# Two float32 transformer blocks on one core: the second mixer's heads, turns and diff chain placed at other chunks and banks

## The chip, the cores and the metric

One NeuronCore of one Trainium2 chip runs the whole program in one launch. The metric is the device time of one execution in microseconds (us). The times shown are those of three executions.

## What is computed

The input is 256 tokens by 2048 columns in float32. A first block (attention and retention, gated and merged, then a gated FFN) is followed by a second one. Cut to what the change touches, the second is:

```python
h = rmsnorm(x, attn_pre_norm)
gq, gk, gv, gg, ga, dq, dk, dv = split(h @ w_in)
o_a = rmsnorm(gla_chunked(gq, gk, gv, log_a), gla_norm) * silu(gg)  # 4 gated heads, 128 by 256
o_b = rmsnorm(diff_attention(dq, dk, dv, lam), diff_norm) * (1 - lambda_init)  # 4 diff heads
x = x + rmsnorm(concat(o_a, o_b) @ w_o, attn_post_norm)
h = rmsnorm(x, ffn_pre_norm)
a, b = split(h @ w_ffn_in)
x = x + rmsnorm((gelu(conv3(a)) * b) @ w_ffn_out, ffn_post_norm)

# diff_attention, each head: (softmax(q1 k1) - lam * softmax(q2 k2)) @ v, causal
```

## The kernel before

The weights are streamed: each block of 512 output columns is eight **chunks** of 512 KB, which SP's queue loads into four slots of `raw`. ACT rounds a chunk to `whi` (L887), DVE subtracts to get the rest `wlo` (L1377), and TensorE multiplies both with the turned activations `hT`, which are held as a high and a low part too (`cols_block`, L377 and L378, or `rows_block` and `tall_block`, L388 to L390, twelve matmuls a chunk in the latter). A slot is free for the next load when DVE has read it, and `whi` is free when TensorE has used the chunk. So ACT and DVE split chunk c+4 right after TensorE has finished chunk c.

All other work is hung into this stream by hand. Every engine has its own program, in which a function `side(c)` or `side(k)` is called after chunk c (or after the split that belongs to it), and `linear_attention(c, h)`, `head_norms(pos)` or `diff_attention(pos)` say by their `if` what happens after which chunk. Nothing is reordered by a scheduler; engines meet at semaphores alone, and an engine that waits in a side holds back the splits or the matmuls that stand behind it.

PSUM has eight banks `ps[:, 0..7]`. The running block owns two or four of them, and side work has the rest. A **turn** (`turn_group`, L455 on TensorE, L931 or L934 on ACT, L1422 or L1426 on DVE) transposes 256 columns of rows into `hT`; TensorE's turn of a group waits by `evicted` until DVE is through with the bank. The eight groups of the second mixer's output (`turn_group(5, ...)`) are four from the gated heads, done in bank 2 (the fourth in bank 0), and one from each diff head, in bank 3.

- A gated head (`linear_attention`) has two halves, t = 0 and 1: decay sums on TensorE (L750), `Exp` on ACT, products on DVE (L1820), scores on TensorE (L757), masked and summed by DVE (L1829 to L1833, the copy L1837 last). Heads 0 to 2 lie beside the blocks `gg0`, `gv1`, `gg1`, head 3 beside the first `dv` block, one chunk later. `linear_out` (L772) multiplies with the values, `norm_gla` and `head_out` scale the head's rows.
- A diff head (`diff_attention`), pos counting chunks from the second `dv` block on: scores (L813) at pos 2+4h, top on DVE, `Exp` on ACT (L1268) at 3+4h, probabilities on DVE (L1901 to L1910) at 4+4h, their turn (L803) at 6+4h, output (L826) at 7+4h, its norm on ACT and DVE (L1879) at 8+4h and 9+4h, its turn at 10+4h. From pos 8 on this lies beside the output projection `o2`.
- Rows are scaled late: `late_scale` on DVE makes a diagonal of token scales (L1448) at k = 3, and TensorE spreads it with one product (L492 in the first block, L468 elsewhere) after chunk 5. It needs a `Sqrt` on ACT (`root`, L966), for which ACT first loads a table.
- The attention heads' norms (`head_norms`, L523, ACT L1003, DVE L1520 to L1528) stand after chunks 1, 5, 9 and 13 of the two `va` blocks.
- At the entry of the last FFN DVE adds the normed mixer rows to `resid` (L1994, in four pieces) before each pair of turns, with `m_gain` (L1930) ahead of pieces 2 and 3.

## Time and profile before

| | |
|---|---|
| median of three runs | 2634.39 us (2633.48 to 2635.44) |
| the profiled execution | 2634.3 us, span 2632.5 us |
| busy share of the span | PE 99%, PEld (weight loads) 87%, DVE 60%, ACT 50%, POOL 2% |
| granted TensorE clock, mean | 0.997 of full |
| chain that ended last | PE 95%, DVE 2%, ACT 2% |
| DMA | 192 GB/s read over the span, 62.8% of the 16 engines' span in the main queue |

"Busy" is the time in which at least one instruction of the engine was under way. Matmuls overlap, since each one's record reaches over the start of the next. The chain of waits is followed back from the last instruction to whatever released each step.

### The profile page before, as it was taken

The numbers are of one execution on the slowest core, as the hardware profiler recorded it, in microseconds if no ns is written. First come the engines' busy times: TensorE is split into PE (matmuls) and PEld (weight loads), VectorE is DVE, ScalarE is ACT, GpSimd is POOL, SyncE is SP. The second block draws the span as 40 slices with busy tenths as digits, with TensorE's granted clock in tenths as the row PEclk, the third lists the DMA queues.
The fourth block names the chain that finished last, engine by engine and source line by source line (L and its number), as shares of the span: only waits on it lengthen the run. The fifth ranks groups of instructions, "written<-read, shape, count | busy, mean of one in ns | idle before, by whom it ended". The sixth has DMA issues, their size and how long they took to land.

```text
span 2632.5 us, 37229 instructions
## 1 busy us (share of the span) xinstructions
PE 2593.8 (99%) x13324; PEld 2291.8 (87%) x13324; DVE 1582.7 (60%) x1682; ACT 1310.1 (50%) x1543; POOL 50.8 (2%) x45
## 2 busy tenths in 40 slices
PE   8999999999999999999999999998999999999998
PEld 7988888888888888888888888897889999998887
DVE  5558655556655544545455557666677777766555
ACT  5445655554445444444444455545554444444444
POOL 0000000000000000000000000000000000000000
PEclk9999999999999999999999999999999999999999
DMA  7665665677666666666666655564556666666664
GB/s 237 199 200 174 184 185 173 188 211 226 196 197 191 198 200 195 199 198 199 198 202 202 207 161 165 170 192 128 187 174 203 200 196 199 201 205 202 204 200 159
DMA packets 233270, 507.28 MB, mean 193 GB/s; under 512 B 15829, under 2 KB 18229, under 8 KB 232548
## 3 DMA queue, kind: packets, MB, share of 16 engines
q1 hardware_dynamic: 231712, 499.31, 62.8%
q0 software_dynamic: 1344, 6.81, 0.8%
q8 instruction: 54, 0.88, 0.1%
q14 instruction: 28, 0.23, 0.0%
q10 hardware_dynamic: 132, 0.03, 0.0%
HBM read 504.00 MB, written 2.10 MB: 192 GB/s over the span
## 4 chain that ended last, share of the span: by engine, by line
PE 95%; DVE 2%; ACT 2%; issue 0%; DVEq 0%; ACTq 0%
PE ps L388 21%; PE ps L390 21%; PE ps L389 21%; PE ps L377 19%; PE ps L378 9%; DVE wlo L1377 1%; PE ps L455 1%; ACT whi L887 1%; PE ps L757 0%; PE ps L691 0%; ACT hT L934 0%; PE ps L523 0%; ACT big L959 0%; DVE hT L1426 0%; PE ps L750 0%
## 5 line engine op out<-in xcount | busy, mean ns | idle before, releaser
L1377 DVE TENSOR_TENSOR wlo<-raw,whi 128x1024 fp32r<-128x1024 f32 x944 | 1170.9, 1244 | 984.0 <-ACT whi L887 976.7
L887 ACT ACTIVATE whi<-raw 128x1024 fp32r<-128x1024 f32 x944 | 998.6, 1059 | 1253.3 <-PE ps L390 872.5
L377 PE MATMUL ps<-hT,whi 128*128 128x512 f32 x2304 | 758.0, 383 | 8.1 <-DVE wlo L1377 4.2
L388 PE MATMUL ps<-whi,hT 128*128 128x512 f32 x1792 | 692.8, 387 | 2.7 <-ACT big L992 1.5
L389 PE MATMUL ps<-wlo,hT 128*128 128x512 f32 x1792 | 680.1, 380 | 0.0
L390 PE MATMUL ps<-whi,hT 128*128 128x512 f32 x1792 | 679.9, 379 | 0.0
L378 PE MATMUL ps<-hT,wlo 128*128 128x256 f32 x2304 | 628.0, 273 | 0.0
L377 PEld LDWEIGHTS ps<-hT,whi 128*128 128x128 f32 x2304 | 435.4, 189 | 70.7 <-issue 6.9
L378 PEld LDWEIGHTS ps<-hT,wlo 128*128 128x128 f32 x2304 | 442.3, 192 | 0.1
L388 PEld LDWEIGHTS ps<-whi,hT 128*128 128x128 f32 x1792 | 339.4, 189 | 53.3 <-issue 3.4
L389 PEld LDWEIGHTS ps<-wlo,hT 128*128 128x128 f32 x1792 | 339.5, 189 | 48.8 <-issue 2.6
L390 PEld LDWEIGHTS ps<-whi,hT 128*128 128x128 f32 x1792 | 339.3, 189 | 48.3
L388 PE MATMUL ps<-whi,split_e 128*128 128x512 f32 x832 | 316.4, 380 | 0.2 <-DVE area_d L1713 0.2
L389 PE MATMUL ps<-wlo,split_e 128*128 128x512 f32 x832 | 315.3, 379 | 0.0
L390 PE MATMUL ps<-whi,split_e 128*128 128x512 f32 x832 | 315.3, 379 | 0.0
L388 PEld LDWEIGHTS ps<-whi,split_e 128*128 128x128 f32 x832 | 157.3, 189 | 22.6 <-DVE area_d L1713 0.6
L390 PEld LDWEIGHTS ps<-whi,split_e 128*128 128x128 f32 x832 | 157.2, 189 | 22.3
L389 PEld LDWEIGHTS ps<-wlo,split_e 128*128 128x128 f32 x832 | 157.3, 189 | 22.0
L2104 POOL TENSOR_TENSOR big<-area_d 128x1024 f32 x11 | 34.2, 3111 | 426.8 <-DVE area_d L1457 426.8
L1426 DVE SCALAR_TENSOR_TENSOR hT<-ps,gains,hT 128x256 fp32r<-128x256 f32 x64 | 27.5, 478 | 16.5 <-ACT hT L934 16.5
L934 ACT ACTIVATE hT<-ps,gains 128x256 fp32r<-128x256 f32 x64 | 26.2, 472 | 22.0 <-PE ps L455 21.8
L2015 DVE SCALAR_TENSOR_TENSOR area_d<-temp,conv,area_d 128x256 f32<-128x256 f32 x88 | 36.7, 480 | 0.0
(248 smaller groups left out, 1009.2 us busy)
## 6 DMA issues: line engine op xcount, KB each, us to landing
raw<-w_ffn_in SPq DMA_DIRECT2D x352, 512.0 KB, 3.7
raw<-w_in SPq DMA_DIRECT2D x304, 512.0 KB, 4.3
raw<-w_ffn_out SPq DMA_DIRECT2D x176, 512.0 KB, 4.5
raw<-w_o_ret SPq DMA_DIRECT2D x32, 512.0 KB, 4.5
raw<-w_out SPq DMA_DIRECT2D x32, 512.0 KB, 4.6
raw<-w_o SPq DMA_DIRECT2D x32, 512.0 KB, 3.7
raw<-w_o_attn SPq DMA_DIRECT2D x16, 512.0 KB, 4.5
resid<-x SPq DMA_DIRECT2D x8, 256.0 KB, 5.9
```

The source lines that it names most:

```text
L377: pe.matmul(acc, whi[:, c % SLOTS, f], in_turn(hT[:, kt, :, :]), start=(kt == 0), stop=False)
L378: mm = pe.matmul(acc[:, 0:SEQ], wlo[:, c % SLOTS, f], in_turn(hT[:, kt, 0, :]), start=False, stop=(kt == KT - 1))
L388: pe.matmul(acc, hi, w_hi, start=start, stop=False)
L389: pe.matmul(acc, hi, w_lo, start=False, stop=False)
L390: return pe.matmul(acc, lo, w_hi, start=False, stop=stop)
L455: mm = pe.transpose(ps[:, bank, k2 * SEQ + t * P:k2 * SEQ + t * P + P], src[:, t, (2 * j + k2) * P:(2 * j + k2 + 1) * P], ident)
L887: act.activation(whi[:, c % SLOTS, :], raw[:, c % SLOTS, :], ACT.Copy).then_inc(hi_ready, 1)
L934: ins = act.activation(dst[:, 2 * j + k2, 0, :], src[:, k2, :], ACT.Copy, scale=gains[:, col0 + 2 * j + k2:col0 + 2 * j + k2 + 1])
L1377: dve.tensor_tensor(wlo[:, c % SLOTS, :], raw[:, c % SLOTS, :], whi[:, c % SLOTS, :].bitcast(F32), ALU.subtract).then_inc(lo_ready, 1)
L1426: ins = dve.scalar_tensor_tensor(dst[:, kt, 1, :], src[:, k2, :], gains[:, col0 + kt:col0 + kt + 1], dst[:, kt, 0, :].bitcast(F32), ALU.mu ...
L2015: ins = dve.scalar_tensor_tensor(dst, src, w, dst, ALU.mult, ALU.add)
L2104: pool.tensor_tensor(hidden[:, bass.ds(4 * i, 4), :], up4, prod, ALU.mult).then_inc(S(f"hidden{u}"), 1)
```

## The change

The arithmetic is the same, and so is the work of each engine, except that ACT loads 38 tables where it loaded 41 in the program's text. What moves:

1. **Root tables ahead.** `root_ready()` is a `Sqrt` of one element, put where ACT loads the table before it is wanted: ahead of the first turn, after the `oa` blocks, and ahead of the last but one `fo` block.
2. **Token scales a chunk later.** TensorE's L492 and L468 come after chunk 6 instead of chunk 5.
3. **`head_norms` a chunk later**, on all three engines (DVE's first `head_squares(0)` stays).
4. **First entry of the second mixer.** ACT and DVE turn groups 0 to 3 in one go, and ACT's squares of pieces 0 and 1 come after them.
5. **Gated heads 2 and 3** do their second half one chunk earlier (`gla_again` is 3 instead of 4), and the last head's `linear_out` comes one chunk earlier, `norm_gla` on ACT two and `head_out` on DVE one.
6. **Diff chain.** Turns of the gated rows at pos 1 to 4 in banks 4 and 5 alternately; scores at 3+4h, turn of probabilities at 7+4h, output at 8+4h, turn of the output at 12+4h in bank 2; the other steps one chunk later too.
7. **Entry of the last FFN.** DVE adds piece 1 to `resid` ahead of two splits, computes the `m_gain` of pieces 2 and 3 after the turn before, and turns group 4 ahead of adding piece 3.

```diff
             return 4 if h < 3 else 0
+
+        def gla_again(h):
+
+            return 4 if h < 2 else 3
         def out_bank(h):
...
                             turn_group(u, src, j, 4 + j % 4, j // 2 + (2 if u == 6 and j else 1), max(0, j - 3))
-                    if u in TURNED_SCALE and c == CPB - 3:
+                    if u in TURNED_SCALE and c == CPB - 2:
                         pe.wait_ge(S("diag"), TURNED_SCALE.index(u) + 1)
                         pe.matmul(ps[:, 4, 0:SEQ], ones, scale_diag, start=True, stop=True).then_inc(S("scale"), 1)
...
+                if c == CPB - 2:
                     pe.wait_ge(S("ones_in"), 16)
                     pe.wait_ge(S("diag"), 1)
                     pe.matmul(ps[:, 4, 0:SEQ], ones, scale_diag, start=True, stop=True).then_inc(S("scale"), 1)
-                if c == CPB - 2:
                     pe.wait_ge(S("gains_in"), 16 * 5)
                     pe.wait_ge(S("lambdas_in"), 16 * 4)
                     turn_gains(16, GAIN_ROWS, 5)
...
             def head_norms(pos):
-                if pos == 1:
+                if pos == 2:
                     pe.wait_ge(acc_freed, base["va"] + 1)
-                if pos % 4 == 1:
+                if pos % 4 == 2:
                     head_sum(pos // 4, 4)
-                if pos == 1:
+                if pos == 2:
...
             def linear_attention(c, h):
-                bank = gla_bank(h)
-                if c in (0, 4):
-                    t = c // 4
+                bank, again = gla_bank(h), gla_again(h)
...
             def diff_attention(pos):
+                if pos == 0:
+                    linear_out(G_HEADS - 1)
                 if pos == 1:
-                    linear_out(G_HEADS - 1)
-                for h in at(pos, 6):
+                    pe.wait_ge(acc_freed, base["dv"] + 2)
+                if 1 <= pos <= 4:
+                    turn_group(5, rows_d, pos - 1, 4 + (pos - 1) % 2, pos, evicted=max(0, pos - 2))
+                for h in at(pos, 7):
                     pe.wait_ge(S("d_p"), h + 1)
-                    pe.wait_ge(S("turned5"), 3)
+                    if h > 1:
+                        pe.wait_ge(S("turned5"), 3 + h)
                     for kt, t in ((0, 0), (0, 1), (1, 1)):
                         mm = pe.transpose(ps[:, 2, kt * SEQ + t * P:kt * SEQ + t * P + P],
                                           diff[:, (t + kt) * P:(t + kt + 1) * P], ident)
                     mm.then_inc(S("d_turn"), 1)
-                for h in at(pos, 2):
-                    if h:
-                        pe.wait_ge(S("turned5"), 4)
-                    else:
-                        pe.wait_ge(acc_freed, base["dv"] + 1)
+                for h in at(pos, 3):
                     for c in range(2):
                         for t in range(NT):
                             mm = pe.matmul(ps[:, c, t * P:t * P + (t + 1) * P], tiles_a[:, 2 * h + c, t * P:t * P + P],
                                            tiles_a[:, 8 + 2 * h + c, 0:(t + 1) * P], start=True, stop=True)
                     mm.then_inc(S("d_score"), 1)
-                if pos in (2, 3, 4):
-                    turn_group(5, rows_d, pos - 2, 2, pos - 1, evicted=pos - 2)
-                if pos == 5:
-                    pe.wait_ge(S("d_top"), 1)
-                    turn_group(5, rows_d, 3, 0, 4)
-                for h in at(pos, 7):
+                for h in at(pos, 8):
                     pe.wait_ge(S("d_pT"), h + 1)
-                    pe.wait_ge(S("turned5"), 4 + h)
                     pe.wait_ge(S("rows5"), 4 + h)
                     v = [dv[:, kt, h * SEQ:(h + 1) * SEQ] for kt in range(NT)]
                     pe.matmul(ps[:, 3, 0:SEQ], dT[:, 0:P], v[0], start=True, stop=True)
                     pe.matmul(ps[:, 3, SEQ:], dT[:, P:SEQ], v[0], start=True, stop=False)
                     pe.matmul(ps[:, 3, SEQ:], dT[:, SEQ + P:], v[1], start=False, stop=True).then_inc(S("d_o"), 1)
-                for h in at(pos, 10):
-                    turn_group(5, rows_d, 4 + h, 3, 5 + h)
+                for h in at(pos, 12):
+                    pe.wait_ge(S("d_pT"), min(h + 2, D_HEADS))
+                    turn_group(5, rows_d, 4 + h, 2, 5 + h)
             def last_gla(c):
                 if c == 1:
...
                     if n == 0:
+                        pe.wait_ge(S("turned5"), 4)
                         acc_free(base["o2"], hc == 1)
                         return
                     for kept in ("m_kept0", "m_kept1"):
...
+            def root_ready():
+
+                act.activation(warm, eps["one"], ACT.Sqrt)
+
             def resid_cols(t, q):
                 return resid[:, t, q * 512:q * 512 + 512]
...
+            act.wait_ge(S("eps_ok"), 1)
+            root_ready()
             act.wait_ge(S("gain_ok"), 1)
             for j in range(2):
                 turn_group(0, j, 4 + j, hT, GAIN["mix"])
                 split(0, j)
             for c in range(2, SLOTS):
...
                     one(2 * i + 2, b + 2 * i + 2, 0)
+                if not last:
+                    root_ready()
                 one(FBLK - 2, b + FBLK - 2, 1)
                 ahead(b + FBLK - 1, last_side, not last)
             def turn_first(k):
-                if k in (5, 6):
-                    for j in (2 * k - 10, 2 * k - 9):
+                if k == 5:
+                    for j in range(4):
                         turn_group(4, j, j, hT, GAIN["pre2"])
-                    squares(4, resid_cols, k - 5, 512, k - 4)
+                if k == 6:
+                    squares(4, resid_cols, 0, 512, 1)
             keep_hidden = feed_in_rows(turn_ahead(3, GAIN["ffn"], 4, (3,)))
             feed_out("fo", 0, False, turn_first, lambda k: keep_hidden(FBLK - 1) if k == 2 else None)
-            turn_gla = turn_ahead(4, GAIN["pre2"], 4, (2, 3))
+            turn_gla = turn_ahead(4, GAIN["pre2"], 4, (1, 2, 3))
             def first_gla(k):
                 turn_gla(k)
...
             def diff_attention(pos):
-                if pos == 2:
+                if pos == 0:
                     norm_gla(G_HEADS - 1)
-                if pos in (2, 3, 4):
-                    turn_group(5, pos - 2, 2, hT)
-                if pos == 5:
-                    turn_group(5, 3, 0, hT)
-                for h in at(pos, 6):
+                if 1 <= pos <= 4:
+                    turn_group(5, pos - 1, 4 + (pos - 1) % 2, hT)
+                for h in at(pos, 7):
                     act.wait_ge(S("d_turn"), h + 1)
                     act.activation(dT[:, 0:SEQ], ps[:, 2, 0:SEQ], ACT.Copy)
                     act.activation(dT[:, SEQ + P:], ps[:, 2, SEQ + P:], ACT.Copy).then_inc(S("d_pT"), 1)
-                for h in at(pos, 10):
-                    turn_group(5, 4 + h, 3, hT)
-                for h in at(pos, 3):
+                for h in at(pos, 4):
                     act.wait_ge(S("d_top"), h + 1)
                     for t in range(NT):
                         for c in range(2):
...
                             ins = act.activation(kept, kept, ACT.Exp, bias=negtop4[:, 2 * t + c:2 * t + c + 1], scale=A_SCALE,
                                                  accum_out=total4[:, 2 * t + c:2 * t + c + 1])
                     ins.then_inc(S("d_exp"), 1)
-                for h in at(pos, 8):
+                for h in at(pos, 12):
+                    turn_group(5, 4 + h, 2, hT)
+                for h in at(pos, 9):
                     norm_heads((S("d_o"), h + 1), "d_sq", "diff", ps[:, 3, :], junk_t)
             def last_gla(k):
...
+                    cs = slice(half * SEQ, half * SEQ + SEQ) if q == 0 else slice(q * 512, q * 512 + 512)
+                    for t in range(NT):
+                        ins = dve.scalar_tensor_tensor(resid[:, t, cs], rows_m[:, t, cs], rstd[:, t:t + 1], resid[:, t, cs],
+                                                       ALU.mult, ALU.add)
+                    ins.then_inc(S("norm_in6"), 1)
                 if q == 1:
                     for c in (2, 3):
                         split(base["ff2"], c)
-                if q >= 2:
-                    m_gain(q)
-                for half in range(2 if q == 0 else 1):
-                    cs = slice(half * SEQ, half * SEQ + SEQ) if q == 0 else slice(q * 512, q * 512 + 512)
-                    for t in range(NT):
-                        ins = dve.scalar_tensor_tensor(resid[:, t, cs], rows_m[:, t, cs], rstd[:, t:t + 1], resid[:, t, cs],
-                                                       ALU.mult, ALU.add)
-                    ins.then_inc(S("norm_in6"), 1)
+
+            def gain_next(j):
+
+                if j in (2, 3):
+                    m_gain(j)
             def conv_sum(blk, i, nth):
                 own(add_low(blk, 0, nth, conv_in[:, :, 2:]))
...
-            feed_in("ff2", 1, turn_ahead(6, GAIN["ffn2"], 0, post_norm), conv_sum, 5, convolve, n_cols)
+            feed_in("ff2", 1, turn_ahead(6, GAIN["ffn2"], 0, post_norm, gain_next, (4,)), conv_sum, 5, convolve, n_cols)

```

The hunks left out do the same on the other engines.

**ACT, start of the program.** Before:

```order
L976 DMA area_g<-k_norm 1x128
L934 ACT_TABLE_LOAD [waits turn0]
L934 ACTIVATE hT<-ps,gains 128x256 [waits gain_ok]
L934 ACTIVATE hT<-ps,gains 128x256
L887 ACTIVATE whi<-raw 128x1024 [waits loaded0]
```

Now:

```order
L980 DMA area_g<-k_norm 1x128
L970 ACT_TABLE_LOAD
L970 ACTIVATE small<-small 128x1 [waits eps_ok]
L934 ACTIVATE hT<-ps,gains 128x256 [waits turn0,gain_ok]
L934 ACTIVATE hT<-ps,gains 128x256
L887 ACTIVATE whi<-raw 128x1024 [waits loaded0]
```

The table load and the small `Sqrt` no longer stand behind the first turn (`turn0`).

**PE, second `dv` block, after its third and fourth chunk** (`big` holds the diff heads' queries and keys, `area_d` the rows that are turned). Before, after the third chunk:

```order
L390 MATMUL ps<-whi,hT 128x512
L813 MATMUL ps<-big 128x128 [waits acc_freed]
L813 MATMUL ps<-big 128x256
L813 MATMUL ps<-big 128x128
L813 MATMUL ps<-big 128x256
L455 MATMUL ps<-first,area_d 128x128 [waits rows5]
L455 MATMUL ps<-first,area_d 128x128 x3
L388 MATMUL ps<-whi,hT 128x512 [waits lo_ready]
```

Now, after the fourth:

```order
L394 MATMUL ps<-whi,hT 128x512
L459 MATMUL ps<-first,area_d 128x128 [waits turned5,rows5]
L459 MATMUL ps<-first,area_d 128x128 x3
L817 MATMUL ps<-big 128x128
L817 MATMUL ps<-big 128x256
L817 MATMUL ps<-big 128x128
L817 MATMUL ps<-big 128x256
L392 MATMUL ps<-whi,hT 128x512 [waits lo_ready]
```

The first scores of a diff head now stand a chunk later and behind the third turn of gated rows; before they stood ahead of the first turn.

**DVE, entry of the last FFN**, from the second turn on. Before:

```order
L1426 SCALAR_TENSOR_TENSOR hT<-ps,gains,hT 128x256
L1377 TENSOR_TENSOR wlo<-raw,whi 128x1024 [waits hi_ready] x2
L1994 SCALAR_TENSOR_TENSOR resid<-big,small,resid 128x512 x2
L1426 SCALAR_TENSOR_TENSOR hT<-ps,gains,hT 128x256 [waits turn_hi6]
L1426 SCALAR_TENSOR_TENSOR hT<-ps,gains,hT 128x256
L1377 TENSOR_TENSOR wlo<-raw,whi 128x1024 [waits hi_ready]
L1930 TENSOR_TENSOR big<-big,area_g 128x2x512 [waits norm_part]
L1994 SCALAR_TENSOR_TENSOR resid<-big,small,resid 128x512 [waits dve_own]
L1994 SCALAR_TENSOR_TENSOR resid<-big,small,resid 128x512
L1426 SCALAR_TENSOR_TENSOR hT<-ps,gains,hT 128x256 [waits turn_hi6]
```

Now:

```order
L1433 SCALAR_TENSOR_TENSOR hT<-ps,gains,hT 128x256
L1998 SCALAR_TENSOR_TENSOR resid<-big,small,resid 128x512 x2
L1384 TENSOR_TENSOR wlo<-raw,whi 128x1024 [waits hi_ready] x2
L1433 SCALAR_TENSOR_TENSOR hT<-ps,gains,hT 128x256 [waits turn_hi6]
L1433 SCALAR_TENSOR_TENSOR hT<-ps,gains,hT 128x256
L1939 TENSOR_TENSOR big<-big,area_g 128x2x512 [waits norm_part]
L1384 TENSOR_TENSOR wlo<-raw,whi 128x1024 [waits hi_ready,dve_own]
L1998 SCALAR_TENSOR_TENSOR resid<-big,small,resid 128x512 x2
L1433 SCALAR_TENSOR_TENSOR hT<-ps,gains,hT 128x256 [waits turn_hi6]
```

The addition to `resid` passed two splits, and L1930 (now L1939) passed a turn.

## Rows read from the trace of the kernel before

**Rows 1.** page, section 1 and the two costliest groups of section 5
```profile
PE 2593.8 (99%) x13324; PEld 2291.8 (87%) x13324; DVE 1582.7 (60%) x1682; ACT 1310.1 (50%) x1543; POOL 50.8 (2%) x45
L1377 DVE TENSOR_TENSOR wlo<-raw,whi 128x1024 fp32r<-128x1024 f32 x944 | 1170.9, 1244 | 984.0 <-ACT whi L887 976.7
L887 ACT ACTIVATE whi<-raw 128x1024 fp32r<-128x1024 f32 x944 | 998.6, 1059 | 1253.3 <-PE ps L390 872.5
```

**Rows 2.** waits of PE, whole span: total us, times, longest
```profile
PE ps L455 <- DVE hT L1422: 4.6, 1, 4.6
PE ps L377 <- DVE wlo L1377: 4.2, 2, 2.8
PE ps L377 <- DVE hT L1426: 1.9, 2, 1.2
PE ps L468 <- DVE temp L1448: 1.8, 2, 1.4
PE ps L523 <- DVE area_d L1520: 1.7, 1, 1.7
PE ps L377 <- DVE temp L1837: 1.7, 1, 1.7
PE ps L455 <- DVE resid L1994: 1.6, 1, 1.6
...
PE ps L388 <- ACT big L992: 1.5, 1, 1.5
PE ps L492 <- DVE temp L1448: 1.5, 1, 1.5
PE ps L826 <- issue: 1.5, 1, 1.5
PE ps L455 <- DVE area_d L1879: 1.2, 1, 1.2
PE ps L388 <- DVE hT L1426: 1.1, 1, 1.1
...
PE ps L757 <- DVE temp L1821: 0.6, 1, 0.6
```

**Rows 3.** timeline of PE, first dv block: start us, length us, engine, line
```profile
1786.04 0.38 PE L390 MATMUL ps<-whi,hT 128*128 128x512 f32 x1
...
1790.79 0.59 PE L772 MATMUL ps<-big,temp 128*128 128x256 f32 x2
```

**Rows 4.** windows: stretch, its length, busy PE PEld DVE ACT POOL, granted clock, DMA, GB/s
```profile
1798.00:1804.00 6.00, 1.42 (x8) 0.96 (x7) 5.29 (x12) 1.85 (x4) 0.00 (x0) 0.87 0.27 87
1804.00:1810.00 6.00, 6.00 (x21) 4.95 (x21) 1.43 (x2) 3.97 (x11) 0.00 (x0) 0.56 0.27 87
```

**Rows 5.** timeline of ACT, the first two instructions that count as busy
```profile
7.10 1.28 ACT L934 ACT_TABLE_LOAD   x1 [7.10 <-PE ps L455]
8.39 0.84 ACT L934 ACTIVATE hT<-ps,gains 128x256 fp32r<-128x256 f32 x2
```

**Rows 6.** timelines of PE and DVE, third gated head
```profile
1655.35 0.46 PE L388 MATMUL ps<-whi,hT 128*128 128x512 f32 x1
...
1658.58 0.29 DVE L1833 TENSOR_TENSOR temp<-big 128x128 f32<-128x128 f32 x1
```

**Rows 7.** timeline of DVE and chain (ACT), steps of a diff head
```profile
1800.62 1.14 DVE L1889 SCALAR_TENSOR_TENSOR area_g<-first,small,ps 128x256 f32<-128x256 f32 x2
...
1802.85 0.17 DVE L1894 TENSOR_SCALAR small<-small 128x4 f32<-128x4 f32 x1
...
1812.62 0.17 DVE L1901 RECIPROCAL small<-small 128x4 f32<-128x4 f32 x1
...
1813.77 0.75 DVE L1910 SCALAR_TENSOR_TENSOR temp<-area_g,small,temp 128x128 f32<-128x128 f32 x2
...
1821.63 1.76 ACT area_g L1268 x8
```

**Rows 8.** timeline of DVE, entry of the last FFN
```profile
1926.13 2.36 DVE L1377 TENSOR_TENSOR wlo<-raw,whi 128x1024 fp32r<-128x1024 f32 x2
```

69 lines of the change are left out of this document (36 added, 33 removed).

## The prediction, made before the changed kernel was run

> **What bounds the kernel.** I read the page first, then the waits of PE, then the timelines around each wait. On the page TensorE is busy for 2593.8 of 2632.5 us, while ACT and DVE, which split the weights, are idle for 1253 and 984 us before those splits, ACT's longest releaser being PE itself [rows 1]. So the matmul stream sets the time, and what can be won are the places where it stands still. The waits of PE list them, and they are the list of the change's parts: nearly always a late DVE or ACT step of side work, 24.9 us in these rows, 28 with the shorter ones [rows 2]. No transfer is in that list. Two things must be added to the listed times. First, a matmul's record is 0.38 us long but the next one starts after 0.216 us: from 1786.04 to the side work at 1790.79 there are 22 of them [rows 3]. So each listed idle stretch began 0.17 us earlier than it shows, and its loss is the listed time plus 0.17. The same rows give a chunk of twelve: 2.6 us. Second, in the 4.6 us wait at 1799 the granted clock falls, to 0.56 of full from 1804 to 1810, between the levels 2.4 and 1.2 GHz [rows 4]. TensorE had done nothing for 4.6 us before. The lost 0.44 of those 6 us is 2.6; I take 2.4, the part in which matmuls ran. The waits of up to 1.7 us cost no clock in these rows.
>
> The profiled execution took 2634.3 us (span 2632.5), the median of the runs is 2634.39: the same. I sum against 2634.3. About 0.2% (5 us) is what a measurement of this kernel can tell from no change.
>
> **The change, part by part.** Every part delays or advances side work against a stream that goes on; nothing is computed less, but three table loads. The price of a part is the wait it had, less the wait it leaves.
>
> *Start.* ACT's first table load of 1.28 us begins at 7.10, released by the first turn, and stands between it and everything else [rows 5]. ACT has nothing to do before. Loaded ahead it costs nothing there: the whole load lies in front of data that come anyway. The first matmul waits 2.8 us for its split [rows 2]; it will wait 1.3 less. **-1.3.** The bounds are 0 (the first weights come no earlier) and 1.3.
> The load ends at 8.38 and the next ACT instruction starts at 8.39 [rows 5], so a load costs 1.28. The Trainium skill (ScalarE: Activation LUTs, What ACT_TABLE_LOAD costs) says 1283 ns and a drain of 1380 ns besides, 2.66 in all; by that the start would give 2.7, which is a rival below.
>
> *Token scales.* L492 waits 1.5, L468 1.8 in two places [rows 2]. The diagonal is ready 1.7 us or less after TensorE asks for it, and the product now comes a chunk of 2.6 us later. What comes behind, the copy on DVE and the wait before the block's end, has the last chunk for cover, 2.6 us against a copy of 0.4 and one split of 1.24; without that chunk as cover it would cost some 0.5. First block: 1.5 + 0.17, **-1.6** (bounds -1.7 and -0.9). The others are in their entries below.
>
> *Head norms.* L523 waits 1.7 for DVE's squares; one chunk later they are long there: **-1.9**. Behind it the last head's scaling ends after DVE's last split of the `va` blocks instead of before, 1.4 us later, and the attention's scores have about 1 us to spare; bound: a new wait of 0.5.
>
> *First FFN entry.* 1.1 + 0.17 for turned rows, behind a table load of 1.28 us. Without the load the split and the turn behind it come 1.28 earlier, but the turn in front of them then holds: I leave 0.3. **-1.0**, bounds 0 and -1.3.
>
> *Second mixer's entry.* L377 waits for turned rows 0.7 of the 1.9 (the longest, 1.2, is at the last FFN) and L468 1.4. ACT's four turns now come ahead of its squares (two of 0.62 us and their reads, 1.25), so DVE's last turn is 1.1 us earlier. The three squares that remain go into the next block in place of two and a table load, 1.25 for 1.28, which is no more work per chunk. 0.9 + 1.6: **-2.4**, bounds -0.9 and -2.5.
>
> *Gated heads.* TensorE waits 1.7 for DVE's last copy (L1837) of head 2 and 0.6 before the scores of head 3 [rows 2]. Both will go: the chain starts a chunk earlier, and head 3's products are ahead of `head_out`. But the second decay sums wait for `g_sT`, that is, for the masks of the first half, and now have one chunk for it instead of two. For head 2, TensorE's chunk starts at 1655.35 and ends 2.67 us later, at 1658.0; DVE, which first has its split, ends the masks' last sum at 1658.87 [rows 6]. A new wait of **0.9**, and the same for head 3. So 1.84 + 0.77 - 1.8: **-0.8**. Bounds: -2.6 and +0.5.
>
> *Diff chain.* The listed waits are 4.6 (a turn for the turn two before it in the same bank), 1.5 (the banks of `dv`, behind ACT's exponentials), 1.5 (L826, marked issue: it waits for DVE's turn, in the same bank), 1.2 (L1879) and 0.2 [rows 2]. With 0.17 each and the clock's 2.4 they are 12.3 us. I lay out the new order from the start of the second `dv` block, in us. TensorE: a chunk and the last gated head's output to 3.9; three chunks with turns and the first scores to 14.3; a fourth with its turn to 17.3; three more to 25.1, where it wants the first probabilities. DVE is through with split and turn at 15.7, then needs 2.4 for the tops [rows 7], 18.1. ACT has its split and turn of that chunk until 18.7, a load of 1.28 and exponentials of 1.8 [rows 7]: 21.9. ACT's next split 1.06 and DVE's 1.24 [rows 1] come first: 24.2. The probabilities take 1.9 [rows 7]: 26.1. TensorE waits **1.0** there. For the later heads the same steps have a chunk more room; by the same laying out the fourth head waits 0.3, the last turn 0.5 for the last scaled rows, since DVE now has it behind two copies and a split. The turns alternate banks and wait for nothing. Left: 1.8. **-10.5**. Bounds: -12.3, and -5 if each of the four heads waits 1.8.
>
> *Last FFN entry.* The waits are 1.6 (L1994), 1.2 and 0.3; with the drains and small ones below the list, 4.4. The first goes: DVE's 2.36 us of splits [rows 8] now stand behind the addition for which TensorE's turn waits. After it DVE has per chunk a split of 1.24, a turn of 0.87, an addition of 1.4 and a product of 1.2, 4.7 for a chunk with turn of 3.1, in either order, so it remains late. I lay it out as above and get waits of 0.4, 0.4, 0.25 and 0.45: 1.5 left. **-2.8**, bounds -1 and -4.
>
> Sum: 1.3 + 1.6 + 1.9 + 1.0 + 2.4 + 0.8 + 10.5 + 2.8 = 22.3. 2634.3 - 22.3 = **2612.0 us**.
>
> **Rivals.**
> 1. *The diff chain pays half.* Every step of a head moves by one chunk, so the chain from scores to probabilities is as long as before, and it is the length that makes a wait. For: my laying out ends with DVE and ACT late by 1.0 already at the first head. Against: the turns of gated rows no longer stand between, and the later heads have more room. Four waits of 1.8 leave 7.2 where I have 1.8: 2617.4; with the last FFN's entry gaining 1 only, 2619.2. Chance 0.14.
> 2. *A table load costs more than its record.* The start, where nothing else is in the way, would give back more than the record's 1.28, if ACT drained before or after. By the rows the next instruction follows at once [rows 5], so a rest could only lie hidden in that instruction or before the load. At most another load's length, 1.3: 2610.7. The Trainium skill (ScalarE: Activation LUTs) has this as its drain; by its 1.38 it is 2610.6. Chance 0.05.
> 3. *Slower: ACT's turn holds DVE.* At pos 12+4h ACT turns the head's output after load and exponentials, 3.1 us, and DVE waits for it with the weights' splits behind. Splits are three chunks ahead, 7.8 us; I find DVE idle for 2.5. It decides if each of the four heads makes TensorE wait 5 us: then the clock falls too, as now at 1804, and a head costs 5.0 + 0.17 + 2.4 = 7.6. Four are 30.3 in place of 12.3 that go: 2634.3 - 11.8 - 12.3 + 30.3 = 2640.5. Against it: 2.5 is far below 7.8. Chance 0.03.
> 4. *No change, the stream of weights takes over.* If SP's loads were just in time, every wait that goes would come back as a wait for weights. For: the main queue is at 63%. Against: ACT and DVE are idle most of the time before their splits, released by PE [rows 1], and PE lists DVE's splits only at the very start. The time would be 2632 to 2636. Chance 0.05.
>
> **How the numbers follow.** The forecast has 0.73. Its own range is 2607 to 2617: I leave waits of 0.3 + 1.8 + 1.8 + 1.5 = 5.4, and they may not occur or be twice as long. Rivals 1 and 2 lie at 2610 to 2619. With the bounds of the start (1.3), the token scales (0.7) and the first FFN entry (1.0) on top of 2617 it is 2620.4, and below, the second entry and the start by rival 2 give another 1. So the range is 2606 to 2621. Faster by over 0.2%: 0.73 + 0.14 + 0.05 = 0.92, within 0.2%: 0.05, slower: 0.03.
>
> **What would show it.** PE's waits would lose L523, L492, both L468, the wait for the last copy, and the 4.6; the clock would stay at 1.00 around 1800. They would gain two of 0.9 at L753 for `temp` (right for the gated heads), one of about 1.0 at L811 for the first probabilities, and waits of 0.3 to 0.5 at the turns of the last FFN's entry. The first whole matmul would start at about 10.3 instead of 11.6. If L811 waits more than 1.5 at several heads, rival 1 holds; if ACT's wait for `raw` or PE's for `wlo` appears in the middle of the kernel, rival 4. The sum is wrong if the total of PE's waits is not near 11 us.

## The result, and the profile after the change

| | before | after |
|---|---|---|
| median of four runs | 2634.01 us (2633.48 to 2635.44) | 2609.89 us (2609.57 to 2610.24) |
| profiled execution, its span | 2634.3, 2632.5 us | 2610.03, 2608.2 us |
| granted TensorE clock, mean | 0.997 | 0.999 |

The ratio after to before is 0.9906, 95% interval 0.9894 to 0.9919: 24.1 us less. I forecast 2612.0 us, 22.3 less.

The page of the changed kernel, its busy times and the two groups that split the weights, which answer [rows 1]:

```profile
PE 2588.5 (99%) x13324; PEld 2289.2 (88%) x13324; DVE 1581.9 (61%) x1682; ACT 1304.7 (50%) x1543; POOL 50.6 (2%) x45
...
L1384 DVE TENSOR_TENSOR wlo<-raw,whi 128x1024 fp32r<-128x1024 f32 x944 | 1170.4, 1243 | 965.6 <-ACT whi L887 957.4
L887 ACT ACTIVATE whi<-raw 128x1024 fp32r<-128x1024 f32 x944 | 997.0, 1057 | 1246.8 <-PE ps L394 871.3
```

Nothing is computed faster. A split lasts what it did, and ACT and DVE are still idle in front of most splits. PE is busy 5.3 us less although it does the same work. The slow clock around 1804 us had stretched some of it by 2.7 (2.4 in the matmuls, 0.3 in the turn ahead of them; see `c_filled`), the list of waits is ten entries shorter, each with 0.17 us of busy tail, and the very first turn's record is 0.3 shorter, which varies from run to run. The rest of the 5.3, 0.6, I can't place. The other 19 us of the 24 were standing still. All listed waits of PE in the changed kernel (engine, line, what it waited for: us in total, times, longest) answer [rows 2]:

```profile
PE ps L381 <- DVE wlo L1384: 3.0, 2, 1.6
PE ps L481 <- DVE temp L1481: 1.6, 1, 1.6
PE ps L753 <- DVE temp L1844: 1.5, 2, 0.7
PE ps L860 <- DVEq L1973: 0.8, 1, 0.8
PE ps L811 <- DVE temp L1919: 0.7, 1, 0.7
PE ps L381 <- DVE temp L1848: 0.4, 1, 0.4
PE ps L459 <- DVE area_d L1892: 0.4, 1, 0.4
PE ps L459 <- DVE gains L1492: 0.3, 1, 0.3
PE ps L392 <- DVE area_d L1724: 0.2, 1, 0.2
```

They add up to 8.9 us where there were 28; I had about 11. Gone are the 4.6, the token scales, the head norms, the entries and the 1.7 of the last copy. New are L753 twice (0.73 each, with the 0.17 just the 0.9 that I had), L811 (0.7, I had 1.0), L459 for the last scaled rows (0.4, I had 0.5), and one that I had not: L381 waits 0.4 for the last copy.

The windows that answer [rows 4] (stretch, length, busy PE, PEld, DVE, ACT, POOL, then the granted clock) have the clock at its upper level, 2.4 GHz:

```profile
1798.00:1804.00 6.00, 5.31 (x29) 4.43 (x28) 4.71 (x10) 4.34 (x9) 0.00 (x0) 1.00 0.39 136
1804.00:1810.00 6.00, 6.00 (x29) 5.28 (x28) 3.96 (x7) 3.40 (x11) 0.00 (x0) 1.00 0.53 175
```

ACT's start in the timeline (start us, length us), which answers [rows 5]:

```profile
3.58 1.28 ACT L970 ACT_TABLE_LOAD   x1 [3.58 <-issue]
4.87 0.20 ACT L970 ACTIVATE small<-small 128x1 f32<-128x1 f32 x1
6.80 0.84 ACT L934 ACTIVATE hT<-ps,gains 128x256 fp32r<-128x256 f32 x2 [1.72 <-PE ps L459]
```

**Where the time came from, by place.** Both programs have 12480 matmuls with weights, in the same order. So the start of the n-th in the trace of before, less its start in that of after, is the lead gained up to that place. It grew as follows; the last column is what I forecast.

| up to | lead, us | gained here | forecast |
|---|---|---|---|
| first weight matmul (11.58 became 9.98) | 1.6 | 1.6 | 1.3 |
| end of the first block | 3.4 | 1.8 | 1.6 |
| second `va` block | 5.4 | 2.0 | 1.9 |
| first FFN's entry | 6.5 | 1.1 | 1.0 |
| second mixer's entry | 9.1 | 2.7 | 2.4 |
| gated heads | 9.3 | 0.1 | 0.8 |
| diff chain | 20.8 | 11.6 | 10.5 |
| last FFN's entry and to the end | 24.5 | 3.7 | 2.8 |

This says where time went, not yet which part of the change brought it. The experiments do that, and they correct the table in two places. The first row also holds scatter: over all profiles shown here the first weight matmul starts at 11.22 us on average in the four kernels with the old start (10.90 to 11.58, and the kernel before is the latest), at 9.89 in the ten with the load ahead (9.48 to 10.30). The mean difference is 1.3, the term as forecast; the other 0.3 of the row is chance.

### The profile page after: what moved, and what is told of

Same layout as the page of the kernel before. It is cut to its first block, busy times and chain, and to the rows that moved or that the text cites. A ratio compares the mean times of both kernels' runs of the same rounds, so it can differ in the third digit from the quotient of the medians.

```text
span 2608.2 us, 37234 instructions
## 1 busy us (share of the span) xinstructions
PE 2588.5 (99%) x13324; PEld 2289.2 (88%) x13324; DVE 1581.9 (61%) x1682; ACT 1304.7 (50%) x1543; POOL 50.6 (2%) x45
## 4 chain that ended last, share of the span: by engine, by line
PE 97%; DVE 2%; ACT 1%; issue 0%; DVEq 0%; ACTq 0%
PE ps L392 21%; PE ps L394 21%; PE ps L393 21%; PE ps L381 19%; PE ps L382 10%; PE ps L459 1%; DVE wlo L1384 0%; PE ps L694 0%; ACT whi L887 0%; PE ps L753 0%; PE ps L760 0%; PE ps L526 0%; PE ps L817 0%; PE ps L549 0%; PE ps L588 0%
## 5 line engine op out<-in xcount | busy, mean ns | idle before, releaser
L381 PE MATMUL ps<-hT,whi 128*128 128x512 f32 x2304 | 758.0, 383 | 3.7 <-DVE wlo L1384 3.0
L381 PEld LDWEIGHTS ps<-hT,whi 128*128 128x128 f32 x2304 | 435.4, 189 | 65.9 <-issue 4.4
L394 PEld LDWEIGHTS ps<-whi,split_e 128*128 128x128 f32 x832 | 157.2, 189 | 22.3
L909 ACT ACTIVATE area_d<-ps 128x1024 f32<-128x1024 f32 x36 | 36.6, 1016 | 0.0
```

The costliest lines, as they stand in the source:

```text
L381: pe.matmul(acc, whi[:, c % SLOTS, f], in_turn(hT[:, kt, :, :]), start=(kt == 0), stop=False)
L394: return pe.matmul(acc, lo, w_hi, start=False, stop=stop)
L909: act.activation(halves(lo.rearrange("p (f t) -> p f t", f=4)), halves_of(ps[:, 4 * par:4 * par + 4, SEQ:]), ACT.Copy)\
```

## The experiments

Each kernel was timed in five rounds, beside the kernel before on the same chip, and that one's median lay between 2633.8 and 2634.4 us. The changed kernel's 2609.89 us comes from another session, so a difference to it of about half a microsecond is not shown by medians alone. The intervals behind the ratios are wide, 2 to 4 us to either side, and most theories lie closer together than that. What tells them apart is whether the single runs overlap, and the traces: the lead by place and the lists of waits.

### One part of the change at a time, put into the kernel before

**`p_start`: only the first table load moved** (its main lines; the wait for `eps_ok` moves with them).

```diff
+            act.wait_ge(S("eps_ok"), 1)
+            root_ready()
             act.wait_ge(S("gain_ok"), 1)
```

> The kernel before with one root table load moved ahead of the first turn (step Start) and nothing else. Kernel before: 2634.0 us. Theory A (a load costs its record, 1.28 us, and the first turn's matmuls run 0.3 shorter, as the changed kernel's first weight matmul at 9.98 in place of 11.58 shows): -1.6, 2632.4 us, and the first ACT reading after the load starts within 0.05 us of the load's end. Theory B (a load also drains the engine for about as long again, with the drain hidden from the records): -2.7 or more, 2631.3 us. Theory C (the first weight chunk's arrival sets the start): 0, 2634.0 us. A lead of 1.6 us at the first weight matmul that is lost again before the end of the first block would say that another wait (the token scale's product, 1.5 us) takes it: then the kernel's time falls by less than 0.5 although the first matmul comes 1.6 earlier.

Measured: 2630.60 us (2630.05 to 2631.61) against 2634.04, ratio 0.9987 (0.9978 to 0.9996). That is 3.4 less, twice A's 1.6, and by the time alone it would speak for B. The trace says otherwise. The first ACT instruction after the load starts 0.01 us behind its end, so no drain shows there. The lead is 1.7 at the first weight matmul and 2.8 behind the first block, since PE's wait for the diagonal shrinks too. Waits of PE, this kernel:

```profile
PE ps L492 <- DVE temp L1453: 0.4, 1, 0.4
```

It was 1.5 in [rows 2]. The timeline of ACT tells why. Before, ACT loads the root's table in front of L966, late in the first block:

```profile
31.36 1.28 ACT L966 ACT_TABLE_LOAD   x1
32.66 0.30 ACT L966 ACTIVATE small<-small 128x2 f32<-128x2 f32 x1
```

With a root as the very first function, the table that it brings also serves the turns and squares that follow, and no load stands in front of the same line. The next load in this kernel comes at 232.5 us, and there are 54 in its trace where there were 55:

```profile
29.42 0.20 ACT L959 ACTIVATION_READ_ACCUMULATOR big<-resid 128x1 f32 x1
29.84 0.30 ACT L966 ACTIVATE small<-small 128x2 f32<-128x2 f32 x1 [0.23 <-DVE small L1467]
```

The Trainium skill (ScalarE: Activation LUTs, Table sets: the hidden batching unit) has a rule that fits: cheap functions, copy among them, stand in every set beside one expensive anchor. The trace agrees for the copies of the turns; the squares, which that list doesn't name, run behind the root's load without another too.

So one moved line took two waits for a load off the path: 1.28 at the start and 1.1 (1.5 less 0.4) at the token scale. Of the rest, 0.4 us comes with the first turn, whose record was between 0.66 and 1.12 us in the profiles of kernels with the old start; it varies from run to run. And the lead grows by 1.0 more around the slow clock, 0.2 of it at the turn at 1804 and 0.8 up to 1809 us, where the lower level held for fewer matmuls than in the profile of before. No part of that comes from the load as far as I can see.

**`p_lead`: all parts ahead of the gated heads.** Its edit is items 1 to 4 of the change, with nothing of 5 to 7.

> The kernel before with everything of the change that lies ahead of the gated heads: start, token scales a chunk later, head norms a chunk later, and both entries; gated heads, diff chain and the last FFN's own entry as before. Theory A (waits add up, each part is worth its own): what the changed kernel's weight matmuls had gained on the old ones when the gated heads began is 9.1 us, and the token scale of the last FFN's entry adds up to 0.5: 2634.0 - 9.1 to 9.6 = 2624.4 to 2624.9 us. By my terms (1.3 + 1.6 + 1.9 + 1.0 + 2.4) it would be 2625.8. Theory B (time won early is given back at later waits which end on transfers): the lead at 1590 us is 9.1 but under 8 at the end, 2626 us or more.

Measured: 2623.86 us (2623.59 to 2624.48), ratio 0.9960 (0.9947 to 0.9974): 10.2 less. B falls: the lead is 9.3 at 1798 us and never shrinks behind it. A holds in kind, with more than its 9.1 to 9.6: the lead grows by 0.6 at the last FFN's entry, and by 1.05 between 1806 and 1809 us, where the lower clock of the 4.6 us wait, which this kernel still has, again ended after fewer matmuls. My five terms, 8.2, were low.

**`p_heads`: gated heads and diff chain alone** (items 5 and 6).

> The kernel before with the gated heads' and the diff chain's new places alone. Theory A: gated heads give 0.0 and the diff chain 11.7, as the distances between the same weight matmuls in both traces say: 2622.3 us; of it 2.4 is the clock, which stays at 1.00 between 1798 and 1810 us. By my terms (0.8 + 10.5) it is 2622.7. Theory B (rival 1, the diff chain pays half): 2627 us. Theory C (part of the 11.7 came only because the parts in front moved ahead): above 2623.5 us.

Measured: 2622.86 us (2622.66 to 2623.14), ratio 0.9956 (0.9942 to 0.9969): 11.2 less, next to my 11.3 and 0.5 short of A's 11.7; its trace gains 11.7 from behind the start on. Rival 1 (2627) is out, and so is C.

**`p_last`: the last FFN's entry alone** (item 7).

> The kernel before with the last FFN's entry reordered alone (its token scale's product stays a chunk earlier, with its own wait of about 0.4 us). Theory A: 3.6 us in the traces less the token scale's 0.4 to 0.6 is 3.0 to 3.2: 2630.8 to 2631.0 us. My term was 2.8 with the scale's wait in it, which would be 2631.7 or more. Theory B (DVE stays late whatever the order, and only the first wait of 1.6 goes): 2632.2 us.

Measured: 2631.21 us (2630.04 to 2632.57), ratio 0.9989 (0.9980 to 0.9998): 2.8 less. Its runs scatter by 2.5 us, so this time can't tell A from my term. The trace can: from 1900 us on the lead grows by 3.3, and of the waits there (1.6, 1.2, 0.3) none is left in its list. So B is out.

The three parts give 10.2 + 11.2 + 2.8 = 24.2, the whole change 24.1. So they add within what can be measured: no wait of a size that would show came back elsewhere. That the two sums agree to 0.1 is luck. The runs of `p_last` alone scatter by 2.5 us, and the 1.05 us at the slow clock in `p_lead` can't be gained again where that slow clock is gone.

### The mechanisms

**`c_filled`: the wait kept, TensorE kept busy.**

```diff
+                if pos == 3:
+                    pe.wait_ge(acc_freed, base["dv"] + 2)
+                    for _ in range(18):
+                        pe.matmul(ps[:, 4, :], la_hi[:, 0:P], sums_r[:, 0:512], start=True, stop=True)
                 if pos in (2, 3, 4):
                     turn_group(5, rows_d, pos - 2, 2, pos - 1, evicted=pos - 2)
```

> The kernel before, with 18 products of 512 columns (la_hi by sums_r, into a bank that nobody reads) put on TensorE in the 4.6 us in which it waits ahead of the second row turn of the diff chain. They take 18 x 0.216 = 3.9 us, so the turn still starts when its bank is free. Theory A (the standing still itself costs 4.6, and the clock that falls after it another 2.4): the granted clock stays at 1.00 from 1798 to 1810 us and the time is 2634.0 - 2.4 = 2631.6 us. Theory B (the clock falls for another reason than the idle TensorE, or the 2.4 is not worth that in time): 2634.0 us with the clock low again in that stretch. If the products take longer than the wait and push the turn, it is slower than 2634.0.

Measured: 2632.98 us (2632.21 to 2634.70) against 2633.82, ratio 0.9998 (0.9989 to 1.0007). The clock part of theory A is shown. These windows stand against [rows 4] (0.87 and 0.56). The products are the only work added, and the turn comes at about the same time:

```profile
1798.00:1804.00 6.00, 5.53 (x26) 4.32 (x24) 5.06 (x12) 2.10 (x4) 0.00 (x0) 1.00 0.30 87
1804.00:1810.00 6.00, 6.00 (x32) 5.34 (x33) 2.25 (x3) 5.17 (x12) 0.00 (x0) 1.00 0.28 90
```

The price is not: the time, 0.8 less with runs that overlap, lies between A's 2.4 and B's nothing and doesn't differ surely from either. In the trace the slow clock had cost 2.7 us, 0.36 in the turn and 2.4 in the twelve matmuls behind it, and all of that comes back. But the next wait of TensorE grows. Its row in this kernel, then the same step in the kernel before:

```profile
1814.85 1.58 PE L813 MATMUL ps<-big 128*128 128x128 f32 x8 [1.19 <-DVE hT L1426]
```

```profile
1816.31 1.58 PE L813 MATMUL ps<-big 128*128 128x128 f32 x8 [0.24 <-DVE hT L1422]
```

1.0 of 2.7 is given back, since DVE's turn does not come earlier when only TensorE is faster. The trace keeps 1.7 at this place, the medians 0.8. The cost of the clock is thus won back in full only where the waits behind it go too, as they do in the change.

**`b_onebank`: the changed kernel, four row turns in one bank.**

On TensorE (ACT and DVE take the same bank):

```diff
-                    turn_group(5, rows_d, pos - 1, 4 + (pos - 1) % 2, pos, evicted=max(0, pos - 2))
+                    turn_group(5, rows_d, pos - 1, 4, pos, evicted=max(0, pos - 1))
```

> The changed kernel (2609.9 us) with all four turns of the gated rows in one bank, each waiting for the one before to be read out, as before the change; all places are the changed kernel's. Theory A (the 4.6 us wait went because norm, head output and tops no longer stand between two turns; the second bank is worth little): the turns stand at 1782.8, 1785.9, 1788.9 and 1793.2 us, and the one before each is read out by 1786.0, 1790.0 and 1792.1, so they wait 0.3, 1.3 and 0.0 us: 1.6 in all and no fall of the clock, 2611.5 us. Theory B (the alternating banks are what removed the wait): the 4.6 with its 2.4 of clock comes back, 2616.9 us. Theory C (later waits swallow it): 2609.9 us.

Measured: 2611.44 us (2610.97 to 2611.57), ratio 0.9914 (0.9901 to 0.9928): 1.5 more than the changed kernel, as A has it (1.6). The list of waits has one new line:

```profile
PE ps L459 <- DVE hT L1429: 0.8, 1, 0.8
```

So the second bank is worth about 1.5 us (1.3 in the trace), and it is not what removed the 4.6 us wait and its clock. They went with the new places. In the kernel before, ACT's norm with its table load, DVE's head output and its tops ([rows 7], 1800.62) lay between the first turn and its reading by DVE, for which the second one waited (timelines of ACT and DVE):

```profile
1796.73 1.28 ACT L1224 ACT_TABLE_LOAD   x1
```

```profile
1798.36 0.17 DVE L1842 RECIPROCAL small<-small 128x2 f32<-128x2 f32 x1 [1.11 <-ACT small L1224]
...
1802.92 0.69 DVE L1422 TENSOR_TENSOR hT<-ps,hT 128x512 fp32r<-128x512 f32 x1
```

**`d_turn11`: the diff heads' output turned a chunk earlier, in bank 3.**

On TensorE (ACT and DVE move likewise, and the waits that guard banks 2 and 3 are put to match):

```diff
-                for h in at(pos, 12):
-                    pe.wait_ge(S("d_pT"), min(h + 2, D_HEADS))
-                    turn_group(5, rows_d, 4 + h, 2, 5 + h)
+                for h in at(pos, 11):
+                    turn_group(5, rows_d, 4 + h, 3, 5 + h)
```

> The changed kernel with the turn of each diff head's output a chunk earlier (11+4h) and in bank 3, where the outputs themselves are, so one chunk behind its rows and in the same bank as before the change. Before it cost a wait of 1.2 us for the scaled rows and one of 1.5 us of the output for the turn ahead of it in the bank. Theory A (the 1.5 was a clash of two sides with no chunk between them, pos 14 and 15 at the end of an o2 block, and only the wait for the rows, 1.2 + 0.17, comes back, while the last turn's 0.4 + 0.17 goes): 2609.9 + 0.8 = 2610.7 us. Theory B (bank 3 is the cause of both): 2609.9 + 2.5 = 2612.4 us.

Measured: 2617.33 us (2616.16 to 2617.81), ratio 0.9936 (0.9923 to 0.9950): 7.4 more. Two runs, the profiled one with them, took 2616.2 us at the changed kernel's mean granted clock, 0.999; the other three took 2617.3 to 2617.8 at 0.998. So 6.3 us go with the waits (6.0 by the lead of the matmuls), and the rest goes with a lower clock in some runs. Both theories fall. Waits of PE:

```profile
PE ps L459 <- DVE area_d L1890: 5.8, 3, 2.9
```

Three of the four heads wait for their scaled rows: 1.4, 1.5 and 2.9 us. The output's wait for a turn in the same bank (L826's 1.5 before) does not appear, and the rows are what ends each wait. So the distance between rows and turn is the cause as the trace has it; 11+4h in bank 2 was not run. The three stand at pos 15, 19 and 23. At the end of an `o2` block, at 15 and 23, two sides follow each other with no chunk between them, so that "one chunk later" is there no time at all; in the kernel before the same step fell on pos 14 and 22. But that isn't the whole cause, since the wait at 19, inside a block, is as long as the one at 15. The chain of waits through the one at pos 19, which ends at 1847.14 us (start us, length us, what), shows what TensorE waits for:

```profile
1843.60 0.30 ACT small L1231
1843.89 0.96 ACT whi L885
...
1844.87 1.23 DVE wlo L1382
...
1846.21 0.89 DVE area_d L1890 x2
...
1847.14 0.66 PE ps L459 x4
```

A split on ACT and one on DVE, 2.2 us, lie between ACT's root and the rows. The place 12+4h covers them, 11+4h doesn't. I had read this part of the change as the two listed waits, 2.7 us; given the other new places it carries 6.0 in the trace.

**`g_head2`: gated head 2 back at its old chunk.**

```diff
-            return 4 if h < 2 else 3
+            return 4 if h < 3 else 3
```

> The changed kernel with the second half of gated head 2 back at its old chunk (head 3 as changed). Theory A (moving it a chunk earlier exchanged one wait of 1.7 us at the start of the dqk blocks for one of 0.73 at the second decay sums and one of 0.41 at the same place as the old one): 1.7 + 0.17 - 0.73 - 0.17 - 0.41 - 0.17 = +0.4, 2610.3 us, and the listed wait for the last copy is 1.6 to 1.7 again. Theory B (my term, without a rest at the copy): +1.0, 2610.9 us. Theory C (the move was worth nothing or did harm): 2609.5 to 2609.9 us.

Measured: 2610.34 us (2609.97 to 2610.44), ratio 0.9910 (0.9895 to 0.9925): 0.45 more, but its runs overlap with the changed kernel's, and by the lead of the matmuls the place costs 0.2. B's 1.0 is out, and A's 0.4 is not told from nothing by the time. The waits have changed as A has it: L753 waits once instead of twice, and the last copy is late by the old amount:

```profile
PE ps L381 <- DVE temp L1848: 1.6, 1, 1.6
```

**`l_splits`: DVE's two splits ahead of the addition again.**

```diff
+                if q == 1:
+                    for c in (2, 3):
+                        split(base["ff2"], c)
                 for half in range(2 if q == 0 else 1):
```

> The changed kernel (2609.9 us) with one part of the last FFN's entry undone: DVE splits two chunks ahead of adding piece 1 to the residual again, instead of behind; the later m_gain and the turn ahead of piece 3 stay. Theory A (this order alone removed the wait of 1.6 us for the residual, 1.6 + 0.17): +1.8, 2611.7 us, and the wait of 1.6 stands again at the second pair of turns. Theory B (DVE is late in this entry by a fixed amount of work, so that what it does not wait at this turn it waits at a later one, and vice versa): under +0.8, 2610.7 us at most. Theory C (the two splits come first and all later turns are then late as before): +3, 2612.9 us.

Measured: 2611.67 us (2611.51 to 2611.95), ratio 0.9913 (0.9900 to 0.9927): 1.8 more, exactly A. In the changed kernel the addition stands ahead of the splits of [rows 8] (timeline of DVE):

```profile
1905.22 1.41 DVE L1998 SCALAR_TENSOR_TENSOR resid<-big,small,resid 128x512 f32<-128x512 f32 x2
1906.54 2.35 DVE L1384 TENSOR_TENSOR wlo<-raw,whi 128x1024 fp32r<-128x1024 f32 x2
```

**`t_scales`: the changed kernel with the scales' product back behind chunk 5.**

```diff
-                    if u in TURNED_SCALE and c == CPB - 2:
+                    if u in TURNED_SCALE and c == CPB - 3:
```

The first block's product (L492 before) moves back in the same way.

> The changed kernel (2609.9 us) with the product that spreads the token scales back behind chunk 5 in all three places. Start, head norms, entries and the rest stay as changed. In the kernel with the early table load alone the first block's wait for the diagonal was 0.43 instead of 1.51 us, so part of my term of 1.6 for the first block belonged to the load. Theory A (each place pays what it waits when the rest of the change is there: 0.43 + 0.17 in the first block, 1.4 + 0.17 at the second mixer's entry, 0.3 + 0.17 at the last FFN's): +2.7, 2612.6 us. Theory B (at the second mixer's entry the squares after the turns and the table load that went already made the diagonal early, so that only the first block and the last FFN pay): +1.1, 2611.0 us. My terms as priced (1.6 in the first block, 1.6 at the second entry): +3.2 or more, 2613.1 us.

Measured: 2611.95 us (2611.61 to 2612.11), ratio 0.9915 (0.9902 to 0.9929): 2.1 more, between A (2.7) and B (1.1). Against the changed kernel's matmuls it loses 0.73 in the first block, 0.60 at the second mixer's entry and 0.41 at the last FFN's, 1.7 in all. Two of its waits are listed:

```profile
PE ps L496 <- DVE temp L1460: 0.4, 1, 0.4
...
PE ps L472 <- DVE temp L1460: 0.3, 1, 0.3
```

Of the 1.4 at the second entry [rows 2] only 0.3 is left even at the old chunk: there too the diagonal is early already by the other parts, the turns without squares between them and one table load less.

### The waits that the change left

**`i_read`: a narrower wait.** The second decay sums overwrite a bank of which DVE needs only the first of four steps.

```diff
+                    elif t:
+                        pe.wait_ge(S("g_read"), 2 * h + 1)
                     else:
-                        pe.wait_ge(S("g_sT"), 3 * h + t)
+                        pe.wait_ge(S("g_sT"), 3 * h)
...
                     act.wait_ge(S("g_sum"), 2 * h + int(k > 0) + 1)
+                    if k:
+                        act.wait_ge(S("g_sT"), 3 * h + 1)
...
                                           masks_m.rearrange("p (n c) -> p n c", n=2), ALU.mult))
+                    dve.sem_inc(S("g_read"), 1)
```

> The changed kernel with a narrower wait at the gated heads: the second decay sums wait only until DVE has read the bank they overwrite (its masks' product, the first of four steps) and not for the sums behind it; ACT's exponential, which overwrites what those sums read, waits for them instead. Theory A (both waits of 0.73 at the decay sums, with 0.17 each, go and nothing takes their place): -1.8, 2608.1 us. Theory B (the exponential is now the late one, and the scores two chunks on, or the last copy at the start of the dqk blocks, wait that much longer): 2609.2 to 2609.9 us.

Measured: 2608.34 us (2607.67 to 2608.53), ratio 0.9900 (0.9885 to 0.9915): 1.6 less than the changed kernel. L753 is off the list, and the wait for the last copy is 0.5 instead of 0.4, which is a part of the missing 0.2.

**`i_all`: four edits at the waits left.** With `i_read`'s, and the second hunk on ACT and DVE too:

```diff
-                for h in at(pos, 5):
+                for h in (0,) if pos == 4 else at(pos, 5) if pos > 5 else ():
...
-                for h in at(pos, 12):
+                for h in (D_HEADS - 1,) if pos == 25 else at(pos, 12) if pos < 24 else ():
...
-                    linear_attention(k, h)
+                    if h < 2 or k != 5:
+                        linear_attention(k, h)
                     if k == 4 and h:
                         head_out(h - 1)
+                    if h == 2 and k == 4:
+                        linear_attention(5, h)
```

> The changed kernel with four edits at the waits that it left: the narrower wait of the second decay sums (-1.8); DVE computes the first diff head's probabilities ahead of a split instead of behind (-0.69 - 0.17); the last diff head's output is turned a chunk later (-0.41 - 0.17); DVE does head 2's last masks and copy ahead of a split (-0.41 - 0.17). Theory A (four independent waits): 2609.9 - 3.8 = 2606.1 us, and of the waits between 1640 and 1900 us none over 0.2 is left. Theory B (the two edits that let DVE wait for ACT ahead of a split make the split late, and TensorE waits for wlo in their place): 2607.5 us or more, with waits for wlo near 1663 or 1805 us.

Measured: 2606.17 us (2605.74 to 2606.41), ratio 0.9892 (0.9877 to 0.9908), A's 2606.1. It is 3.7 below the changed kernel (28.2 below the one before in its session, where the change has 24.1), and its runs don't overlap with those of the changed kernel. The whole list of PE's waits:

```profile
PE ps L381 <- DVE wlo L1388: 3.0, 2, 1.6
PE ps L481 <- DVE temp L1485: 1.6, 1, 1.6
PE ps L862 <- DVEq L1981: 0.8, 1, 0.8
PE ps L459 <- DVE gains L1496: 0.3, 1, 0.3
PE ps L392 <- DVE area_d L1728: 0.2, 1, 0.2
```

Between 1640 and 1890 us nothing is left. Letting DVE stand for ACT ahead of a split cost nothing, as the splits are three chunks ahead of their use.

## Why the prediction was right, and where its steps were off

- **The frame held.** The matmul stream sets the time, each listed wait costs its length plus 0.17, and waits add. The last was an assumption, and the three parts (24.2 against 24.1) bear it out within their scatter. `l_splits` (1.6 + 0.17 forecast, 1.8 measured) and `i_all` (3.8, 3.7) show the price of a single wait.
- **Start, 1.3, and token scales, 1.6: sum right by luck, attribution wrong.** The two gave 3.4 where I had 2.9, and 0.3 of that is the scatter of the start. But the load moved ahead is worth 2.4 by itself (1.28 and 1.1), and the scale's product a chunk later only 0.7 when the load is gone. The failing step is "loaded ahead it costs nothing there": I counted the load of the start and did not look which later load it would make needless. That load was the one behind which the diagonal came late.
- **Head norms, 1.9, and first FFN entry, 1.0.** Measured 2.0 and 1.1. The wait of 0.3 that I left at the latter does not appear.
- **Second mixer's entry, 2.4.** Measured 2.7. Here too the scale's later place gives 0.6 and not the 1.6 that I gave it. The other 2.1 comes with the turns ahead of the squares and the table load gone; no run parts those two.
- **Gated heads, 0.8: the one term that failed.** Measured 0.1. The two new waits were foreseen and priced right (0.73 + 0.17 each). "Both will go" was wrong: the wait for the last copy shrank from 1.7 to 0.4 instead of going. The timelines of ACT and DVE in the changed kernel, at the place of [rows 6] and just behind it, show the chain:

```profile
1655.47 1.28 ACT L1233 ACT_TABLE_LOAD   x1
```

```profile
1657.09 0.17 DVE L1853 RECIPROCAL small<-small 128x2 f32<-128x2 f32 x1 [1.11 <-ACT small L1233]
...
1659.35 1.23 DVE L1384 TENSOR_TENSOR wlo<-raw,whi 128x1024 fp32r<-128x1024 f32 x1
1660.49 1.22 DVE L1840 TENSOR_TENSOR big<-ps,masks 128x1024 f32<-128x1024 f32 x1
...
1663.14 0.28 DVE L1848 COPY temp<-ps 128x128 f32<-128x128 f32 x1
```

  DVE idles 1.1 for ACT's load, then does head 1's output and a split, and only then the masks, whose copy ends at 1663.42. Head 2's half had moved a chunk, but `head_out(1)` and its load had not.
- **Diff chain, 10.5.** Measured 11.6. My layout of the first head was good: 1.0 forecast, 0.7 measured. The trace, ACT and DVE in the changed kernel, has the steps of [rows 7]:

```profile
1795.05 1.28 ACT L1273 ACT_TABLE_LOAD   x1
```

```profile
1801.49 0.75 DVE L1919 SCALAR_TENSOR_TENSOR temp<-area_g,small,temp 128x128 f32<-128x128 f32 x2
```

  The waits left are 0.7 + 0.4 plus 0.17 each, 1.4 in place of my 1.8, and the fourth head doesn't wait. That explains 0.4 of the 1.1. Another 0.3 is the slow clock, which I priced at 2.4 for the matmuls without the turn that it stretched too. The last 0.4 is in no listed wait, and I have not found it. What I had not seen is which edit carries the sum: not the alternating banks (1.5), but the distance between the scaled rows and their turn (6.0 in the trace if taken back).
- **Last FFN's entry, 2.8.** (4.4 less 1.5 is 2.9; I took 2.8.) Measured 3.7, of which 0.4 is the scale's place. The first wait was priced right (`l_splits`). Of the 1.5 that I left in four waits, none reached 0.2 us.
- **Rivals.** 1 (half of the diff chain) fell with `p_heads`. 2 (the load's drain): each of the 52 loads in the trace of the changed kernel starts 0.02 us behind the instruction ahead of it (the first has none ahead), the next instruction starts 0.01 behind its end, and the start gave back 1.3 on average; the extra 1.1 of `p_start` had another place and cause. By the Trainium skill (ScalarE: Activation LUTs, What ACT_TABLE_LOAD costs) 1.38 more should have come with each load; no trace here shows it. 3 (ACT's turn holds DVE) did not occur. 4 (the stream of weights takes over) is out to 2606 us: PE's waits for `wlo` stand in the first 16 us alone.

## What to carry to other kernels

When a fixed stream sets the time, price each edit by the wait it removes, lay out what the *next* late producer is, and expect such waits to add; but look for the load or the norm that several of them share, because then one edit pays twice and the other hardly. Count distance in real work between two steps, not in positions of a schedule: the splits of other engines lie in it too, and where two positions follow each other with nothing between, a step moved by one gains nothing. Here one position less between rows and turn, at four heads, cost 6 us. A clock that fell after a wait is worth its full loss only if the waits behind it go as well.

## What was unexpected of the hardware

The clock fell after the 2.8 us wait at the start in some executions and not in others. The wait was 2.77 us in the profile of before and 2.84 in those of `p_last`, `p_heads` and `c_filled`, which all have the old start. The granted clock from 12 to 16 us was 1.00 in the first two, and in `p_heads` and `c_filled`:

```profile
12.00:16.00 4.00, 4.00 (x18) 3.60 (x17) 1.16 (x3) 2.10 (x4) 0.00 (x0) 0.57 0.97 338
```

```profile
12.00:16.00 4.00, 4.00 (x19) 3.67 (x18) 1.12 (x3) 2.06 (x4) 0.00 (x0) 0.61 0.95 332
```

Both were left 0.3 us behind the profile of before at 17 us, though their first weight matmuls were 0.5 and 0.7 ahead of it; the next wait (1.48 us without the fall) took up a part of the loss. In the profile of `d_turn11` a wait of 2.90 us left the clock at 1.00, and so did all waits of up to 1.7 us that I looked at. In the ten profiles with the load ahead the wait at the start is 1.6 us or less, and the clock is 1.00 throughout from 8 to 20 us: the early load also spares the fall that some executions had there. So of the waits near 3 us two in five were followed by the lower level, and the one of 4.6 us was in each of the four profiles with it; `c_filled`, where TensorE was kept busy, has no such wait.

How much the fall cost differed as well, behind the same wait of 4.6 us. The first twelve matmuls behind the turn, from the start of the first to the start of the last, took 4.8 us in the profile of before, 4.7 in `p_last`, 4.0 in `p_start` and 3.8 in `p_lead`, against 2.5 in `c_filled` at full clock. So one profile's 2.4 us is the upper end of what the fall cost these twelve matmuls, 1.3 to 2.4 us.
